# Operands M1, M7 and M6 of the gate and up products: their row sums formed by pairs of transposes in PSUM

## What is computed

```python
x = x + rms_norm(mix_out, norm_mix_post[l])
h = rms_norm(x, norm_ffn_pre[l])
gate = causal_dwconv(jnp.einsum("btd,df->btf", h, ffn_w_gate[l]), ffn_conv_w[l], ffn_conv_b[l])
up = jnp.einsum("btd,df->btf", h, ffn_w_up[l])
ffn_out = jnp.einsum("btf,fd->btd", jax.nn.gelu(gate, approximate=True) * up, ffn_w_down[l])
x = x + rms_norm(ffn_out, norm_ffn_post[l])
```

## Time and profile before

| | us |
|---|---|
| median of 3 runs | 2846.29 |
| the three runs | 2846.11, 2846.29, 2850.65 |
| the profiled execution, its own time | 2849.86 |
| its span in the trace | 2848.2 |

### The profile page before, as it was taken

How to read it: one execution, slowest core, us unless ns; L and a number is a source line. 1 busy time by engine, 2 the same in 40 slices (tenths; PEclk the granted TensorE clock), 3 DMA queues, 4 the chain that set the end, 5 groups by cost and what they waited for, 6 DMA issues and landing times.

```text
span 2848.2 us, 37816 instructions
## 1 busy us (share of the span) xinstructions
PE 2801.0 (98%) x13851; PEld 2366.2 (83%) x13851; DVE 1667.0 (59%) x1855; ACT 1230.2 (43%) x1465; POOL 353.9 (12%) x417
## 2 busy tenths in 40 slices
PE   7999999999999999999988999999999999999998
PEld 6888888888888888888877888888888888888887
DVE  4232333244333333443567887888878778878788
ACT  3233443333222222222455555555555555555554
POOL 1000000000000000000000122222222222222213
PEclk9999999999999999999999999999999999999999
DMA  5333333332223334434644588888888888888876
GB/s 187 89 89 103 89 96 95 112 103 89 91 87 92 91 97 135 155 123 147 205 138 130 159 180 178 160 181 176 159 181 175 162 180 174 161 183 171 162 176 239
DMA packets 451575, 405.93 MB, mean 143 GB/s; under 512 B 13087, under 2 KB 357283, under 8 KB 448433
## 3 DMA queue, kind: packets, MB, share of 16 engines
q1 hardware_dynamic: 397664, 295.73, 34.2%
q0 software_dynamic: 49232, 100.86, 21.3%
q10 hardware_dynamic: 4608, 8.39, 0.8%
HBM read 304.26 MB, written 100.66 MB: 142 GB/s over the span
## 4 chain that ended last, share of the span: by engine, by line
PE 95%; DVE 2%; ACT 1%; issue 1%; DMA 0%; POOL 0%; DVEq 0%; SPq 0%; POOLq 0%; ACTq 0%
PE ps L921 19%; PE ps L608 18%; PE ps L925 10%; PE ps L611 9%; PE ps L833 6%; PE ps L958 5%; PE ps L959 5%; PE ps L960 5%; PE ps L632 4%; PE ps L634 4%; PE ps L633 4%; PE ps L878 1%; PE ps L1020 0%; PE ps L1022 0%; PE ps L752 0%
## 5 line engine op out<-in xcount | busy, mean ns | idle before, releaser
L1650 DVE TENSOR_TENSOR w_lo<-raw,w_hi 128x2048 fp32r<-128x2048 f32 x128 | 293.4, 2292 | 553.1 <-ACT w_hi L1065 553.0
L1606 POOL DMA_DIRECT2D down_sums<-arena x304 | 262.2, 971 | 906.1 <-ACT arena L1363 882.1
L1065 ACT CAST w_hi<-raw 128x2048 fp32r<-128x2048 f32 x128 | 244.0, 1906 | 252.1 <-PE ps L634 195.0
L2033 DVE TENSOR_TENSOR sum_ring<-quads 128x1024 f32<-128x1024 f32 x166 | 203.4, 1225 | 171.5 <-PE ps L925 137.5
L1319 ACT CAST op_ring<-sum_ring 128x1024 fp32r<-128x1024 f32 x166 | 174.7, 1053 | 271.8 <-DVE sum_ring L2033 271.8
L608 PE MATMUL ps<-h_hi,w_hi 128*128 128x512 f32 x1152 | 281.3, 397 | 1.1 <-ACT w_hi L1065 1.1
L611 PE MATMUL ps<-h_hi,w_lo 128*128 128x512 f32 x1152 | 272.9, 389 | 0.0
L608 PE MATMUL ps<-h_lo,w_hi 128*128 128x512 f32 x1152 | 272.8, 389 | 0.0
L921 PE MATMUL ps<-hl,op_ring 128*128 128x512 f32 x1064 | 266.9, 393 | 3.6 <-ACT op_ring L1319 2.5
L608 PEld LDWEIGHTS ps<-h_hi,w_hi 128*128 128x128 f32 x1152 | 217.5, 191 | 48.3 <-ACT w_hi L1065 1.5
L608 PEld LDWEIGHTS ps<-h_lo,w_hi 128*128 128x128 f32 x1152 | 216.2, 188 | 44.9
(11 more groups left out here) (334 smaller groups left out, 4645.7 us busy)
## 6 DMA issues: line engine op xcount, KB each, us to landing
raw<-in_w_in SPq DMA_DIRECT2D x88, 1024.0 KB, 5.3
down_sums<-arena POOLq DMA_DIRECT2D x320, 256.0 KB, 6.7
quads<-in_ffn_w_gate SPq DMA_DIRECT2D x88, 512.0 KB, 4.8
quads<-in_ffn_w_up SPq DMA_DIRECT2D x88, 512.0 KB, 4.7
quads<-in_ffn_w_down SPq DMA_DIRECT2D x88, 512.0 KB, 7.9
raw<-in_w_out SPq DMA_DIRECT2D x24, 1024.0 KB, 5.0
merge_gates<-arena ACTq DMA_DIRECT2D x32, 256.0 KB, 2.0
raw<-in_w_up_a SPq DMA_DIRECT2D x8, 1024.0 KB, 5.3
```

Of the source, the lines that this page charges most:

```text
L1065: act.copy(w_hi[:, s, :], raw[:, s, :]).then_inc(hi_ready, 1)
L1606: pool.dma_start(dst, src, accum_op=ALU.add).then_inc(acc_added[s], 16)
L1650: dve.tensor_tensor(w_lo[:, s, :], raw[:, s, :], f32(w_hi[:, s, :]), ALU.subtract).then_inc(lo_ready, 1)
L2033: dve.tensor_tensor(op_sum[slot_of(i, pos)], quads[:, a, :], quads[:, b, :], ALU.subtract if q in (M7, M6) else ALU.add).then_inc(ff_sum, 1)
```

## The change

The three pairs of DVE additions for M1, M7 and M6 are gone, and `sum1` with them. In their place `turn_pieces` takes two slices of `x_rows` for these operands and transposes both, piece by piece, into the same 128 columns of PSUM. The first of the two starts the group and the second adds to it. The wait for `h_sum` gives way to one for `xn_ready`, which says that all four tiles are normalised. M7 and M6 read unchanged rows of `x_rows`, since no sum is written back any more. ACT, POOL and SP have the same instructions in the same order.

```diff
                 elif q == M1:
-                    pe.wait_ge(h_sum, 5 + n)
-                    rows = sum1[:, n, :]
+                    rows = (x_rows[:, n, LEFT], x_rows[:, 2 + n, RIGHT])
                 elif q == M7:
-                    pe.wait_ge(h_sum, 7 + n)
-                    rows = x_rows[:, n, RIGHT]
+                    rows = (x_rows[:, n, RIGHT], x_rows[:, 2 + n, RIGHT])
                 else:
-                    pe.wait_ge(h_sum, 9 + n)
-                    rows = x_rows[:, 2 + n, LEFT]
+                    rows = (x_rows[:, n, LEFT], x_rows[:, 2 + n, LEFT])
+                if q in (M1, M7, M6):
+                    pe.wait_ge(xn_ready, 2 + TT + 4)
+                else:
+                    rows = (rows,)
                 for j in range(HALF):
-
-                    mm = pe.matmul(ps[:, TURN_BANKS[r] + j // 4, (j % 4) * P:(j % 4 + 1) * P], rows[:, j * P:(j + 1) * P],
-                                   ident[:, :], start=(j % 4 == 0), stop=False, is_transpose=True, skip_group_check=True)
+                    for s, part in enumerate(rows):
+
+                        mm = pe.matmul(ps[:, TURN_BANKS[r] + j // 4, (j % 4) * P:(j % 4 + 1) * P],
+                                       part[:, j * P:(j + 1) * P], ident[:, :], start=(j % 4 == 0 and s == 0), stop=False,
+                                       is_transpose=True, skip_group_check=True)
                 mm.then_inc(turned2, 1)
...
             lo(0, 2)
-            for n in range(2):
-                dve.tensor_tensor(sum1[:, n, :], x_rows[:, n, LEFT], x_rows[:, 2 + n, RIGHT], ALU.add).then_inc(h_sum, 1)
             lo(0, 3)
             weight_sum(0, 4)
-            dve.wait_ge(h_sum, 6)
-            for n in range(2):
-                dve.tensor_tensor(x_rows[:, n, RIGHT], x_rows[:, n, RIGHT], x_rows[:, 2 + n, RIGHT], ALU.add).then_inc(h_sum, 1)
             lo(0, 4)
-            for n in range(2):
-                dve.tensor_tensor(x_rows[:, 2 + n, LEFT], x_rows[:, n, LEFT], x_rows[:, 2 + n, LEFT], ALU.add).then_inc(h_sum, 1)
             weight_sum(0, 5)
```

More of the change, by code:

```diff
@@ L238, in build @@
         diff3 = ar(0, 2 * D2).rearrange("p (n d) -> p n d", n=2)
-        sum1 = ar(32, 2 * D2).rearrange("p (n d) -> p n d", n=2)
         Q = HALF * P
```

## The result

The changed kernel takes 2853.19 us, the median of 19 runs (2851.27 to 2855.67), against 2848.93 us for 19 runs of the kernel before (2845.87 to 2850.94). The medians are 4.3 us apart. The ratio of the two sets of runs is 1.0019, with a 95% interval of 1.0013 to 1.0026, or +3.7 to +7.4 us; its middle lies a little above the 1.0015 of the two medians. The slowest run of before is faster than the fastest of after. The profiled execution has a span of 2851.8 us, 3.6 more than before. One run of an experiment further down (M6 only) took 3104.05 us at a mean granted clock of 0.85, a slower state than that of all other runs, and is left out of its median.

What follows compares the result with a forecast made beforehand. A ring of PE and ACT bounds the kernel, with DVE ahead of it. Removed additions 0, added transposes +5.2 and clock -0.3 give +4.9 on the median 2846.3, so 2851.2 us; range 2848 to 2856.

Steps and rivals of the forecast that it cites:

- The removed additions: Three pairs of DVE additions, 7 us in all, worth 0 on the path, since DVE is 4 to 5 us ahead.
- The added transposes: 48 more PE transposes at turns 8 to 13, 0.108 us each, 5.2 us, all on the path.
- the ring: Cycle of PE and ACT alone: turn, `pieces_hi`, `less_hi`, `pieces_rest`, next turn, because PSUM banks are few.
- The clock: PE at 1.2 GHz for part of turn 11 to M6 costs some 2.4 us; part of it may come back.
- the lower bound: Cost of the added transposes if all low-clock stretches go: 5.2 - 2.4 = +2.8 us.
- the 0.3 taken off: Taken from the 5.2 us of added transposes for low clock that may come back, giving +4.9 us.
- product M6 starting about 5 us later than 1510.17: Sign that the forecast is right, on PE's timeline at the end of the first pair's turns.
- The stall: DVE's 4.06 us wait for the third pair's weights moves by the same 5 us and gives nothing back.
- the third rival: DVE, 7 us lighter, gets the third pair's weights loaded earlier; the 4.06 us go: +1.1 us, chance 0.07.
- More time at 1.2 GHz: Rival: runs of 32 transposes drop the clock behind them at M3 and M7: +8.4, 2854.7 us, chance 0.12.
- Adding in PSUM: Rival: the second transpose of each pair waits for the first to drain: +14.4, 2860.7 us, chance 0.06.
- the forecast's "same": Outcome within about 0.2% (5.7 us) of before, given 0.60, against slower 0.36 and faster 0.04.

Runs made afterwards that it cites:

- M6 only: Kernel before with only M6 made by pairs of transposes (turns 12 and 13), M1 and M7 by DVE additions as before: 2849.70 us, ratio 1.0006.
- without additions: Kernel before without the six DVE additions and with single transposes, part of the computation left out: 2848.15 us, ratio 1.0001.
- additions and pairs: Kernel before with its six DVE additions kept and every transpose of M1, M7 and M6 made twice into the same columns: 2853.42 us, ratio 1.002.
- threes: Changed kernel with three transposes for each piece of M1, M7 and M6, the first slice added twice: 2858.99 us, ratio 1.0041.
- those eight apart: Changed kernel with all eight transposes of the first slice ahead of all eight of the second: 2853.47 us, ratio 1.0021.
- more additions: Kernel before with four more 128x1024 additions on DVE ahead of those for M1: 2848.47 us, ratio 1.0004.
- the changed kernel with the copy first: Changed kernel with ACT's copy of product M1 ahead of turn 10's low part and the high part of M7's weights: 2849.58 us, ratio 1.0007.

## Why the prediction was right, and where its steps were off

| kernel | stretch as profiled | at 2.4 GHz | against 25.13 | transposes added |
|---|---|---|---|---|
| without additions | 25.13 | 25.13 | 0 | 0 |
| M6 only | 28.15 | 26.85 | +1.72 | 16 |
| changed | 31.71 | 30.28 | +5.15 | 48 |
| additions and pairs | 31.92 | 30.27 | +5.14 | 48 |
| threes | 37.17 | 35.54 | +10.41 | 96 |

The third column is an estimate: from the stretch as profiled is taken what the run of transposes behind the 2.58 us of idle time lasted above its price at full clock.

**The removed additions: 0.** Right. Taking them away alone leaves the time as it was (+0.3 us, and the same idle times of PE), and adding 4.6 us of them shows how near DVE is: its lead was put at 4 to 5 us and is 3.8.

**The added transposes: 48 x 108 ns = 5.2, all in the ring.** Right: +5.15 in the changed kernel at full clock, linear from 16 to 96. The whole kernels agree: +5.6 and +5.6 for the two experiments with 48, +4.3 for the changed kernel itself, +11.1 for 96. Of the turns only 12 and 13 were tested alone. The 0.15 us that I allowed at most for a turn 12 hidden under ACT's high part of turn 11 doesn't show: 16 transposes at turns 12 and 13 cost 1.72 in full.

**The clock.** This step failed in its sizes. I counted 2.4 us of before as low clock that might come back: 0.44 and 0.4 at turns 11 and 12, 1.6 at M6. For turns 11 and 12 the stretch without additions gives 0.57 in all; that a slower turn 12 is partly hidden under ACT's high part of turn 11 is my reading of why. For M6, the eight matmuls do take 1.5 us more, but little of it reaches the end. From the start of M6 to DVE's sum of the second pair's M7 weights, behind which the first half of the third pair's load is issued, it took 1523.26 - 1510.17 = 13.09 us before (low clock at M6) and 1526.73 - 1513.97 = 12.76 after (full clock): 0.33. PE waits in both for the later stall, and what it loses at M6 it waits less there. PE's wait ahead of the products by the low part (L925 before, L927 after) in the stall is 2.23 us after, where before had 0.99. The changed kernel met the low clock later instead, in a product of 3.65 us behind which no idle time is left, where before had 1.48 us:

```profile
1537.87 1.22 PE L927 MATMUL ps<-h,op_ring 128*128 128x256 f32 x8 [2.23 <-DVE op_ring L2049]
1539.65 3.65 PE L923 MATMUL ps<-h,op_ring 128*128 128x512 f32 x8 [0.56 <-DVE arena L2062]
```

Of the 2.4 us, then, 0.57 + 0.33 = 0.9 were there to come back, and the lower bound of 5.2 - 2.4 = +2.8 should have been +4.3, 1.5 higher. (The upper end of the spread, +6.5, is worked out nowhere in the prediction.) In the changed kernel nothing came back at turns 11 and 12 either: its second run of 32 lost 1.43 us where before had lost 0.57. So the 0.3 taken off had no ground; 5.2 is what the stretches show at full clock. What the sum left out is the low clock of before at turns 5 to 7, ahead of the stretch, though its rows stand in the earlier trace rows. It is why the sign "product M6 starting about 5 us later than 1510.17" came out as 3.8.

**The stall.** That it moves and gives nothing back was right (4.10 for 4.06), but my reading of the chain was not. I took the sum at 1523.26 to wait for a PE product that ended at 1523.16. DVE itself came free only then. And the load that ends the stall is not the one issued at 1524.50 but the second half, issued at 1526.77 behind the sum after next (1525.53, M6's weights). The timeline of DVE before, and a piece of the chain that ended last:

```profile
1521.81 0.74 DVE L2096 SCALAR_TENSOR_TENSOR arena<-arena,prm 128x512 f32<-128x512 f32 x1
1522.59 0.75 DVE L2099 SCALAR_TENSOR_TENSOR arena<-arena,prm 128x512 f32<-128x512 f32 x1
1523.26 1.22 DVE L2033 TENSOR_TENSOR sum_ring<-quads 128x1024 f32<-128x1024 f32 x1
...
1526.77 5.14 DMA quads<-in_ffn_w_gate
```

DVE works nearly without a gap from 1511.09 on, which is behind ACT's low part of turn 13 and the high part of a weight operand. In the changed kernel the same holds from 1514.89 on. DVE is the bound there, as the third rival asked, and yet nothing came back: its dense stretch begins with ACT steps of the ring, behind all that was taken away. That is why the rival failed, not for the reason that I gave. That nothing was given back was right, but by another path than the one I argued.

**The rivals.** More time at 1.2 GHz behind long runs: no. The first runs of 32 and 48 stayed at 1.00, and the products behind every run of 32 or 48 ran at full speed. By the Trainium skill ("TensorE: Matmul & The Clock Gate", Part 4: PE-mode transpose) transposes would not hold the clock up; the trace of the threes disagrees for 5.2 us on end. The page's figure is for bf16 and these runs are in float32, so it is shown for float32 alone. Adding in PSUM: no, 107 to 108 ns whether the second of the two follows the first directly or comes eight later.

**The absolute time.** Forecast 2851.2, measured 2853.2. The difference, +4.9 against +4.3, was not at fault; three runs of before had a median of 2846.3, and 19 have 2848.9. The runs of one kernel lie 5 us apart, and the profiled one was not 3.6 but 0.9 above its kernel's median. That 4.9 lies so near 4.3 is in part luck, since 0.3 was taken off without ground. And the forecast's "same" was a near thing: the change is clear of noise, the ratio of 1.0019 stands just under the 0.2% that I had set as what can be told, and its interval reaches over it.

## What to carry to other kernels

Moving additions from an engine that waits to the one that sets the end costs the full price of what the latter does in their place, however idle it looks in between, as long as the step that ends that idle time itself waits for the work that was added; then the idle time moves and does not shrink. Ask of each idle time of the bounding engine who ended it and what stood ahead of that step in its engine's order; here one line moved in ACT's order was worth 1.8 us of the stretch and about 1.5 us of the kernel, and 7 us taken off DVE were worth nothing. A step that is late at a low clock costs only what the next wait doesn't absorb, so don't count its whole excess as time that may come back.

## What the runs showed of the hardware

- A float32 transpose of 128x128 on PE costs 106 to 108 ns from start to start in a run at 2.4 GHz, though each lasts 0.27 us (270 to 273 ns in the trace of before); the runs of 32 and 48 that fell partly to 1.2 GHz lost 1.4 to 1.7 us.
- The clock can rise from 1.2 to 2.4 GHz while PE does nothing but transpose: in the threes' second run of 48 it was 0.50 from 1502.90 to 1505.90 and 1.00 from 1506.90 to 1508.70.
- Two transposes that add in the same 128 columns of PSUM back to back cost as much as two that don't follow each other: 31.71 and 31.72 us for the stretch.
- After 2.58 us of idle time ahead of turn 11 the low clock set in at the end of that idle time or within the transposes behind it in before, the changed kernel, the pairs with additions, the threes, those eight apart and M6 only, and not in the runs without additions or with more additions. With 1.10 or 0.25 us of idle time there it did not set in, in any of the profiles. At product M6, with 1.10 us of idle time ahead of turn 13's `less_hi` and 1.10 behind it, it set in in five (before, the pairs with additions, the threes, more additions, the changed kernel with the copy first) and not in the other seven. So what decides it is not shown by the idle time alone, and stays open here.
